# Two sums moved to the vector engine, sample rows in four strips, and sample scores padded to 128 rows, in a two-layer decoder trunk

## The reference

```python
shift, scale, gate = split(silu(c) @ w_ada + b_ada, 3)
x = x + gate * rmsnorm(branch(rmsnorm(x, g_pre) * (1 + scale) + shift), g_post)
```

```python
qk  = einsum(q, k) * dmat                        # scores, with decay
num = a * einsum(q, S) + einsum(qk, v)           # state rows and score rows
den = a * einsum(q, n) + sum(qk)                 # the same two parts, summed
h   = num / maximum(abs(den), exp(-m))
hn  = h * rsqrt(mean(h * h) + eps) * g_head
```

## Time and profile before

| | |
|---|---|
| median of 3 runs | 2228.76 us (2226.25 to 2232.56) |
| time of the profiled execution | 2226.1 us |
| its span in the trace | 2224.5 us |
| PE busy | 2144.5 us, 96% of the span |
| DVE, ACT busy | 941.4 us, 676.8 us |
| moved from and to memory | 298.96 MB |

### The profile page before, as it was taken

How to read it: one execution, slowest core, us unless ns; L and a number is a source line. 1 busy time by engine, 2 the same in 40 slices (tenths; PEclk the granted TensorE clock), 3 DMA queues, 4 the chain that set the end, 5 groups by cost and what they waited for, 6 DMA issues and landing times.

```text
span 2224.5 us, 37038 instructions
## 1 busy us (share of the span) xinstructions
PE 2144.5 (96%) x15828; PEld 1866.3 (84%) x15828; DVE 941.4 (42%) x1432; ACT 676.8 (30%) x1137; POOL 75.7 (3%) x126
## 2 busy tenths in 40 slices
PE   5899999999999999997899999999999999999998
PEld 2579989999999856667889999999899999996676
DVE  4344645546465422235433434334243525254224
ACT  4123434435344321225322222222222222223121
POOL 1000000000000100000000000000000000001000
PEclk8899999999999999998999999999999999999999
DMA  8883222232221588854434343453434244519622
GB/s 321 328 286 96 77 61 78 63 92 58 78 59 58 181 309 309 318 198 133 86 79 114 79 114 79 96 87 83 92 100 98 77 88 84 104 59 335 238 81 100
DMA packets 290527, 298.96 MB, mean 134 GB/s; under 512 B 8721, under 2 KB 213769, under 8 KB 288857
## 3 DMA queue, kind: packets, MB, share of 16 engines
q1 hardware_dynamic: 279504, 247.87, 39.7%
q0 software_dynamic: 10576, 48.45, 6.2%
q10 hardware_dynamic: 290, 0.32, 0.1%
HBM read 277.58 MB, written 23.11 MB: 135 GB/s over the span
## 4 chain that ended last, share of the span: by engine, by line
PE 86%; DMA 9%; DVE 2%; ACT 2%; issue 1%; DVEq 0%; ACTq 0%; SPq 0%
PE PJ L913 49%; PE PJ L1197 14%; DMA raw<-in_w_in_mlstm 5%; DMA obuf<-in_w_ada 3%; PE MX L1125 3%; PE PJ L939 3%; PE MX L1054 2%; PE MX L1063 1%; PE MX L1163 1%; PE MX L1077 1%; DMA arena<-in_x_prompt 1%; PE PJ L1219 1%; PE MX L1017 1%; PE MX L1411 1%; ACT w_hi L1472 1%
## 5 line engine op out<-in xcount | busy, mean ns | idle before, releaser
L913 PE MATMUL PJ<-h_hi,w_hi 128*128 128x272 f32 x3200 | 683.0, 295 | 2.4 <-DVE w_lo L1938 2.4
L913 PE MATMUL PJ<-h_hi,w_lo 128*128 128x272 f32 x3200 | 665.3, 290 | 0.0
L913 PE MATMUL PJ<-h_lo,w_hi 128*128 128x272 f32 x3200 | 663.4, 289 | 1.5 <-issue 1.5
L913 PEld LDWEIGHTS PJ<-h_hi,w_hi 128*128 128x128 f32 x3200 | 506.0, 190 | 26.4 <-issue 20.1
L913 PEld LDWEIGHTS PJ<-h_lo,w_hi 128*128 128x128 f32 x3200 | 506.4, 190 | 1.7 <-issue 1.7
L913 PEld LDWEIGHTS PJ<-h_hi,w_lo 128*128 128x128 f32 x3200 | 503.4, 190 | 0.0
L1938 DVE TENSOR_TENSOR w_lo<-raw,w_hi 128x2048 fp32r<-128x2048 f32 x94 | 215.4, 2292 | 305.5 <-ACT w_hi L1472 305.3
L1472 ACT ACTIVATE w_hi<-raw 128x2048 fp32r<-128x2048 f32 x94 | 179.4, 1909 | 57.4 <-DMA raw<-in_w_in_mlstm 42.3
L1197 PE MATMUL PJ<-w_hi,h_hi 128*128 128x512 f32 x448 | 181.5, 405 | 0.0
L1197 PE MATMUL PJ<-w_hi,h_lo 128*128 128x512 f32 x448 | 176.4, 394 | 0.0
L1197 PE MATMUL PJ<-w_lo,h_hi 128*128 128x512 f32 x448 | 176.1, 393 | 0.0
(11 more groups left out here) (396 smaller groups left out, 2231.2 us busy)
## 6 DMA issues: line engine op xcount, KB each, us to landing
arena<-in_w_ada SPq DMA_DIRECT2D x64, 1024.0 KB, 8.8
raw<-in_w_in_mlstm SPq DMA_DIRECT2D x52, 1024.0 KB, 17.1
raw<-in_w_in_attn SPq DMA_DIRECT2D x40, 1024.0 KB, 5.7
obuf<-in_w_ada SPq DMA_DIRECT2D x32, 1024.0 KB, 10.9
raw<-in_w_out_attn SPq DMA_DIRECT2D x16, 1024.0 KB, 12.9
raw<-in_w_out_mlstm SPq DMA_DIRECT2D x16, 1024.0 KB, 5.0
obuf<-in_w_in_mlstm SPq DMA_DIRECT2D x12, 1024.0 KB, 27.2
arena<-in_state_C POOLq DMA_DIRECT2D x8, 1024.0 KB, 15.8
```

Of the source, the lines that this page charges most:

```text
L913: last = mm(PJ[:, 2 * pair + f, 0:HT], w, h[:, k, HT * f:HT * f + HT], start=(k == 0 and n == 0), stop=(k == KT - 1 and n == 2))
```

## The change

- `memory` step 2 on DVE adds the score columns to the state columns of chunks 1 to 3 in `qn`; step 4 on PE then makes the denominators with a product over 128 score columns and one over the 384 summed ones.
- `Ds` becomes 128 rows high, zero below row 32 (one memset in `gate_maxima`), and DVE adds it to `qn[:, TP:T]`.
- After step 5, ACT takes only the left half of the bank, times a mask of the strips' rows, and DVE, in its step 5, adds the right half times the other mask. Step 6 on PE then has one score product and one selecting product for each half, both over 128 rows, and one product for the denominator; it waits on `qs_done`.
- DVE's step 7 first adds the two blocks of squares; step 8 has two products instead of four.
- The 32 sample rows of an output product are laid out in four strips of columns: strip `j` holds column block `j` of each quarter. `sample_sum` and the sample part of `gate_rows` become four products of 128 columns, one for each strip; the latter writes bank 2, so that `strip` waits for `mod_taken` after a gate. Squares and gating of the samples run once per layer over 128 partitions.
- `x_sample`, `g_post` for samples and `y_sample` are moved with four pieces of 512 B for each row instead of one of 2 KB.
- Four semaphores of the first stage become one, with the same order.

```diff
             def strip(landed, j, n):
+                if j == 0 and is_gate(n - 1):
+                    pe.wait_ge(mod_taken, n - 7)
...
             def gate_rows(n):
-                mm(MX[32 * g:32 * g + 32, 1, :], sel[0:MROWS + 1, X_GS:X_GS + TS], rows, start=True, stop=True)\
-                    .then_inc(mod_turned, 1)
+                for j in range(4):
+                    last = mm(MX[32 * j:32 * j + 32, 2, P * g:P * g + P], sel[0:MROWS + 1, X_GS:X_GS + TS],
+                              rows[:, P * j:P * j + P], start=True, stop=True)
+                last.then_inc(mod_turned, 1)
...
             def sample_sum(l, g):
-                mm(MX[32 * g:32 * g + 32, 1, :], sel[:, X_ST:X_ST + TS], scp[:, :], start=True, stop=True)\
-                    .then_inc(ysum_made, 1)
+                for j in range(4):
+                    last = mm(MX[32 * j:32 * j + 32, 1, P * g:P * g + P], sel[:, X_ST:X_ST + TS],
+                              scp[:, P * j:P * j + P], start=True, stop=True)
+                last.then_inc(ysum_made, 1)
...
             def memory(m, p):
-                    mm(MX[:, 2, :], ones, Dm[:, :], start=True, stop=False)
-                    mm(MX[:, 2, P:TP], ones, qn[:, P:TP], start=False, stop=True).then_inc(num_ready, 1)
+                    mm(MX[:, 2, 0:P], ones, Dm[:, 0:P], start=True, stop=True)
+                    mm(MX[:, 2, P:TP], ones, qn[:, P:TP], start=True, stop=True).then_inc(num_ready, 1)
...
-                    pe.wait_ge(qg_done, val(0, 1, m, 1))
+                    pe.wait_ge(qs_done, val(0, 1, m, 1))
                     for blk in range(2):
                         o = MX[:, 3, TS * blk:TS * blk + TS]
-                        mm(o, vs[0:TS, P * blk:P * blk + P], Ds[0:TS, :], start=True, stop=False)
-                        for c in range(2):
-                            mm(o, Dm[:, DV * c + P * blk:DV * c + P * blk + P], fix[:, C_SS + TS * c:C_SS + TS * c + TS],
-                               start=False, stop=(c == 1))
-                    mm(MX[:, 3, 64:64 + TS], ones[0:TS, :], Ds[0:TS, :], start=True, stop=False)
-                    mm(MX[:, 3, 64:64 + TS], ones, qn[:, TP:T], start=False, stop=True)\
-                        .then_inc(nums_ready, 1)
+                        mm(o, vs[:, P * blk:P * blk + P], Ds, start=True, stop=False)
+                        mm(o, Dm[:, P * blk:P * blk + P], fix[:, C_SS:C_SS + TS], start=False, stop=True)
+                    mm(MX[:, 3, 64:64 + TS], ones, qn[:, TP:T], start=True, stop=True).then_inc(nums_ready, 1)
...
-                    pe.wait_ge(hsq_done, val(0, 2, m, 2))
+                    pe.wait_ge(hsum_done, val(0, 1, m, 1))
                     for f in range(2):
-                        for blk in range(2):
-                            last = mm(MX[:, 1 + f, 0:HT], ones, hsq[:, blk, HT * f:HT * f + HT],
-                                      start=(blk == 0), stop=(blk == 1))
+                        last = mm(MX[:, 1 + f, 0:HT], ones, hsq[:, 0, HT * f:HT * f + HT], start=True, stop=True)
...
             def memory(m, p):
-                    fn(Dm, MX[:, 2, :], ACT.Copy).then_inc(qg_done, 1)
+                    fn(Dm[:, 0:DV], MX[:, 2, 0:DV], ACT.Copy, scale=bm[:, NB:NB + 1]).then_inc(qg_done, 1)
...
             def memory(m, p):
+                    dve.wait_ge(P_done, val(0, 1, m, 1))
+                    chain(tt(qn[:, P:TP], qn[:, P:TP], Dm[:, P:TP], ALU.add))
                     cp(nout[:, ds(h + 64, 1)], nn[:, 3:4]).then_inc(S_done, 1)
...
-                    tt(Ds[0:TS, :], Ds[0:TS, :], MX[0:TS, 3, 64:64 + TS], ALU.mult).then_inc(Ps_done, 1)
+                    chain(tt(Ds[0:TS, :], Ds[0:TS, :], MX[0:TS, 3, 64:64 + TS], ALU.mult))
+                    tt(qn[:, TP:T], qn[:, TP:T], Ds, ALU.add).then_inc(Ps_done, 1)
...
+                if p == 5:
+                    dve.wait_ge(qg_done, val(0, 1, m, 1))
+                    stt(Dm[:, 0:DV], MX[:, 2, DV:2 * DV], bm[:, NB + 1:NB + 2], Dm[:, 0:DV], ALU.mult, ALU.add)\
+                        .then_inc(qs_done, 1)
...
                 if p == 7:
+                    dve.wait_ge(hsq_done, val(0, 2, m, 2))
+                    tt(hsq[:, 0, :], hsq[:, 0, :], hsq[:, 1, :], ALU.add).then_inc(hsum_done, 1)
```

More of the change, by code:

```diff
@@ L108 @@
 C_OH, C_O3, C_SS = 305, 313, 337
-C_FIX = C_SS + 2 * TS
+C_FIX = C_SS + TS
 C_NEGD, C_NEGS = C_FIX, C_FIX + 768
@@ L698, in _ @@
                     sp.wait_ge(xs_ready, 2)
-                    for g in range(4):
-                        sp.dma_start(y_sample.rearrange("b t d -> (b t) d")[:, 512 * g:512 * g + 512],
-                                     xs[32 * g:32 * g + 32, :]).then_inc(y_out[1], 16)
+                    for j in range(4):
+                        sp.dma_start(y_sample.rearrange("b t (g j c) -> (b t) j g c", g=4, j=4)[:, j],
+                                     xs[32 * j:32 * j + 32, :].rearrange("p (g c) -> p g c", g=4)).then_inc(y_out[1], 16)
             sp.wait_ge(y_out[0], 16 * 8)
@@ L948, in _ @@
             tr(MX[:, 2, 0:80], gvec, ident[0:80, 0:80]).then_inc(vec_ps, 1)
-            pe.wait_ge(ct_rows, 1)
+            pe.wait_ge(ct_steps, 2)
             for k in range(KT):
                 last = tr(MX[:, 3, NSEQ * k:NSEQ * k + NSEQ], c_rows[:, P * k:P * k + P], ident[0:NSEQ, 0:NSEQ])
-            last.then_inc(ct_ps, 1)
-            pe.wait_ge(ct_ready, 1)
+            last.then_inc(ct_steps, 1)
+            pe.wait_ge(ct_steps, 4)
             def turn_x(t):
@@ L1117, in _, with strip @@
             layer0("l0z", it0, (None, GR - 1))
-            def strip(landed, j):
+            def strip(landed, j, n):
                 at = fixed(pe, landed)
-                pe.wait_ge(ct_ready, 1)
+                if j == 0 and is_gate(n - 1):
+                    pe.wait_ge(mod_taken, n - 7)
+                pe.wait_ge(ct_steps, 4)
                 pe.wait_ge(u_in[j], at)
@@ L1271, in _ @@
             pe.wait_ge(sc_s, 1)
-            for c in range(4):
-                last = tr(MX[:, 0, :].rearrange("p (g c t) -> p g c t", g=4, c=4)[:, :, c, :],
-                          ys[:, P * c:P * c + P], ident)
+            for g in range(4):
+                last = tr(MX[:, 0, P * g:P * g + P], ys[:, P * g:P * g + P], ident)
             last.then_inc(t_samp, 1)
@@ L1456, in _ @@
             act.wait_ge(c_in, 32)
-            fn(c_tanh, c_rows, ACT.Tanh, scale=0.5).then_inc(ct_tanh, 1)
+            fn(c_tanh, c_rows, ACT.Tanh, scale=0.5).then_inc(ct_steps, 1)
             def round_hi(ph, it, e, j=0):
@@ L1526, in _ @@
             row_squares(0)
-            act.wait_ge(ct_ps, 1)
+            act.wait_ge(ct_steps, 3)
             act.wait_ge(const_in, 16)
-            fn(cT[:, 0:KT * NSEQ], MX[:, 3, 0:KT * NSEQ], ACT.Copy).then_inc(ct_ready, 1)
+            fn(cT[:, 0:KT * NSEQ], MX[:, 3, 0:KT * NSEQ], ACT.Copy).then_inc(ct_steps, 1)
             row_root(0)
@@ L1671, in out_square, with sample_square @@
                 act.wait_ge(y_sq, 16 * l + 4 * g + t)
-                act.wait_ge(ysq_s, 4 * l + g + (t > 1))
+                act.wait_ge(ysq_s, l + (g == 3 and t > 1))
                 fn(jk, PJ[:, bank_of(l, t), :], ACT.Square, accum_out=st[:, 4 * t + g:4 * t + g + 1]).then_inc(y_sq, 1)
-            def sample_square(l, g):
-                rows = slice(32 * g, 32 * g + 32)
-                act.wait_ge(ysum_made, 4 * l + g + 1)
-                act.wait_ge(y_sq, 16 * l + 4 * g + 2)
-                fn(jk[rows, :], MX[rows, 1, :], ACT.Square, accum_out=st[rows, 16:17]).then_inc(ysq_s, 1)
+            def sample_square(l):
+                act.wait_ge(ysum_made, 4 * l + 4)
+                act.wait_ge(y_sq, 16 * l + 14)
+                fn(jk, MX[:, 1, :], ACT.Square, accum_out=st[:, 16:17]).then_inc(ysq_s, 1)
             def out_root(l, nth, t):
@@ L2379, in gate_maxima @@
                 chain(dve.memset(Rt[0:GP.stop, :], 0.0))
+                chain(dve.memset(Ds, 0.0))
                 chain(dve.memset(tg[:, 0:1], 0.0))
```

58 lines of the change are left out of this document (27 added, 31 removed).

## The result

The median after is 2192.78 us (2188.76 to 2197.3, four runs) against 2229.94 us of the kernel before beside it (2226.25 to 2232.56, four runs). The ratio is 0.983, with a 95% interval from 0.9807 to 0.9853. The forecast was 2193 us, in a range from 2184 to 2208.

A forecast was written before the change was run, and what follows sets the result against it. PE, at work for 96% of the span, was taken as the bound. Savings of 10.0 + 5.1 + 6.9 + 4.8 + 4.2 = 31.0 us plus 5 for the clock, off the 2228.76 us median, gave 2193 us, range 2184 to 2208.

The forecast's parts named there:

- Step 6: Score and selecting products on PE: 2.36 us become 1.1, saving 10.0 us over eight heads; 7.1 by number of records.
- Step 4: Product over `Dm` on PE: 0.86 us becomes 0.22 over 128 columns, saving 0.64 a head, 5.1 us for eight.
- Step 8: Sums of squares on PE: eight records become four, saving 0.86 us a head, 6.9 us for eight.
- the sign named in the prediction: Heads in the changed trace come 2.7 to 2.8 us closer together, if loads keep up.
- Gates and sample sums: Four narrow products on PE overlap across strips: 0.6 us saved each, 4.8 us for eight gates, 4.2 for seven sums.
- The last sum of `out0`: Sample sum after the last strip, where the residual waits for the `x_prompt` reload: its 0.6 us saving is not counted.
- The sum: All savings of PE time without the clock: 31.0 us, with a low bound of 19.1.
- The clock: Half-speed stretches behind step 6 in three of eight heads mostly go: 5 us saved, bounds 0 and 6.8.
- the rule weighed in the prediction: Throttling follows an idle engine, so step 6 is not the cause; second rival, 2198 us, chance 0.18.
- DVE's covers: New DVE work stays hidden: 1.7 us left ahead of step 6, and 2.48 us against 0.72 ahead of step 8.
- The weight loads: ACT waited for weights in `raw` three times from 1131 to 1990 us, 15.2 us in all, 11.4 once.
- The fourth rival: Layer 1's weight loads become the last wait, so heads can't get shorter: 2220 us, chance 0.08.

The follow-up runs named there:

- scores32: The changed kernel with the two score products of step 6 on 32 rows, as before the change; one execution took 2188.99 us.
- sums_only: The kernel before with only the two sums of steps 4 and 8 moved to DVE; 2215.74 us, ratio 0.9969 to the kernel before.
- one_strip: The changed kernel with the four narrow products of each gate and sample sum all in one strip; one execution took 2196.70 us.
- fold_only: The kernel before with only the folded step 6, the padded scores and the merged semaphores; 2210.53 us, ratio 0.9952 to the kernel before.
- fold_sums: The kernel before with the folded step 6 and the two sums on DVE, without the four strips; 2186.14 us, ratio 0.9807 to the kernel before.
- strips_only: The kernel before with only the sample rows in four strips, steps 2 to 8 as before; 2222.51 us, ratio 0.9987 to the kernel before.
- late_short: The changed kernel with two extra multiplications (1.4 to 1.5 us forecast) on DVE directly before the new addition of step 5; one execution took 2192.81 us.
- late_long: The changed kernel with a long reciprocal (about 3.5 us forecast) on DVE directly before the new addition of step 5; it took 2210.76 us.
- second pair: Repeat traces of both kernels without new edits: the kernel before took 2228.54 us, the changed kernel 2183.03 us (median).
- experiment 5: The changed kernel with the `x_prompt` reload in four pieces, 2180.70 us, ratio 0.9799; beside it both kernels again, changed 2183.03 us (0.9816), before 2228.54 us.
- experiment 6: The run `fold_sums`: the kernel before with the folded step 6 and the two sums on DVE, without strips; 2186.14 us against 2229.70, ratio 0.9807.
- before_again: The kernel before, unchanged, profiled once more; it took 2228.54 us.

## Why the prediction was right

The base, the bound and the mechanism held, and the total, 36 us forecast against 37 measured, is right; that it is so close is partly luck, as told below. By its steps:

- *Step 6*, 1.25 us a head: it is 1.33. The choice between 10.0 and 7.1 us was the choice between two prices of a 32-row group, and `scores32` settled it for the higher.
- *Step 4*, 0.64: distances from step 4 to step 6 shrank by 0.71 (17.94 to 17.23). `sums_only`, which has the shorter sum and the old step 6, shows 0.65 of it (17.30); the rest goes with the fold, whose step 6 no longer begins with a change to 32 rows. *Step 8*, 0.86: from step 8 to the next step 4 it is 0.91. The three make 2.98 us a head, 23.8 in eight, where 22.0 were summed; the sign named in the prediction was 2.7 to 2.8.
- *Gates and sample sums*, 0.6 each: a gate's four products take 0.33 us, a little over the 0.29 read off the twelve narrow ones, and a sum's 0.22; together 4.40 us over seven in `out0` and 5.0 over eight in `out1`, so 0.63 each. `one_strip` shows that it is the overlap. The last sum of `out0` saved nothing, as said: the wait for the reload stands at 4.0 us beside 4.1.
- *The sum*: 33.2 us by distances against 31.0. It was 7% too small, each term a little, step 6 the most: its 1.33 lies above the larger of the two prices, 1.25.
- *The clock*, 5 us, bounds 0 and 6.8. Behind step 6 the granted clock went to 0.50 in 15 of 32 heads of the four profiled kernels with the old step 6 (3, 2, 6 and 4), and in none of 72 heads of the nine profiled kernels with the new one on time. A drop costs a head 1.5 us, so some 6 us an execution. `scores32`, with its 1.47 us of step 6, shows none either. That the old step 6 is the cause is shown by `fold_only` and `fold_sums` against `sums_only` and `strips_only`; what exactly it is about 2.36 us of small products is not. The idle time of the rule weighed in the prediction isn't needed. What counts is the stretch ahead of a fall, which the earlier trace rows does not show: in 13 of the 15 PE is busy for all of it, in the first head of the kernel before as follows (PE, PEld, DVE, ACT, POOL, clock, DMA share, GB/s). In the other two, both a fourth head, it is busy for 2.54 and 2.31 of 3.4 us.

```profile
1161.00:1164.40 3.40, 3.40 (x26) 3.05 (x24) 0.00 (x0) 0.00 (x0) 0.00 (x0) 1.00 0.00 0
1164.40:1167.80 3.40, 3.40 (x16) 3.40 (x17) 0.77 (x3) 1.41 (x3) 0.00 (x0) 0.50 0.00 0
```

- *DVE's covers*: 1.7 us forecast ahead of step 6, 1.77 found; 1.8 forecast ahead of step 8 (2.48 less 0.72), 1.84 found. `late_short` and `late_long` bracket the first from both sides.
- *The weight loads*. The prediction read the earlier trace rows as all of ACT's waits for weights. The same view has one more, 8.0 us for a piece that lands in `obuf`, so four pieces were late and not three. After the change five pieces in `raw` and two in `obuf` are.
- *The fourth rival*, weights of layer 1 as the last wait, may be true of one head. From step 4 of the fourth head to that of the fifth there are 116.6 to 124.9 us in folded kernels and 122.3 to 129.8 in the others, in every execution more than in the heads next to it. Loads issued there need 44.2 us (median) to land in the changed kernel, against 17.3 in the second head. DMA issues of the changed kernel (count, KB each, median us to landing), from 1500 to 1570 and from 1250 to 1320 us:

```profile
raw<-in_w_in_mlstm SPq DMA_DIRECT2D x3, 1024.0 KB, 44.2
```

```profile
raw<-in_w_in_mlstm SPq DMA_DIRECT2D x4, 1024.0 KB, 17.3
```

and its waits from 1131 to 1990 us, for the earlier trace rows:

```profile
ACT w_hi L1471 <- DMA raw<-in_w_in_mlstm: 21.0, 5, 12.4
...
PE MX L1359 <- DVE arena L2430: 2.1, 1, 2.1
PE PJ L913 <- DVE w_lo L1935: 2.1, 1, 2.1
```

  That head gave 0.85 us in the first pair of traces and 5.5 in the second. From the waits it is likely that part of its gain hangs on when those loads land, but no experiment shows it; I priced it as one rival of six and not as a fixture of one head.

What the prediction didn't see is the noise of other stages. In the first pair of traces layer 0 took 4.75 us more after than before, for no reason in the change, and the span shrank by 30.6 us where the stages behind layer 0 show 35.9. In the second pair layer 0 went the other way, and the span shrank by 46.2. The ratios, 0.983 (38 us) here and 0.9816 (41 us) in experiment 5, lie between. Three comparisons have each their own executions of the kernel before: the medians differ by 37 us here, by 44 in experiment 5, and by 44 in experiment 6, which has only two of the three parts. That the forecast met the first to 0.2 us is thus partly luck; what the traces bear out is the sum of its terms.

Open is the strips' share of the median. Their 9.4 us stand in the distances of every kernel that has them. The transition behind them does not give it back: it averages 177.8 us in the eight traces with strips and 178.0 in the six without (`one_strip` among these). Yet no median shows the whole of it.

## What to carry to other kernels

Where the matrix engine is the bound, price a small product by the distance from its start to the next start, and count each change between 32 and 128 rows as a cost of its own; padding to 128 rows was cheaper than being exact. When work moves to another engine, compute the cover from the end of the new work to the start of the waiting one, and note that a wait of 1.5 us on the matrix engine cost as much again through the clock in six of eight heads. Judge parts of a change of 1% by the stage distances of the traces: the times of the parts, each known to within 4 us, added up to half of the whole. When you look for what brought the clock down, read the stretch ahead of the fall and not the slow one.

## What the runs showed of the hardware that was not expected

- In layer 0's attention, where all kernels run the same code, the clock fell in three places 136.5 us apart in six of 14 profiled executions, in one place in one, and in none in seven. A set of three costs some 4.5 us, and both kernels have executions of either kind. PE was busy for all of such a stretch, but not ahead of it: it had waited 1.2 us for DVE. The first fall in `before_again`, and the same place in the trace of the kernel before, which has the wait and no fall:

```profile
190.50:193.90 3.40, 2.33 (x15) 1.27 (x16) 1.02 (x3) 0.00 (x0) 0.00 (x0) 1.00 0.70 184
193.90:197.30 3.40, 3.40 (x18) 3.40 (x17) 2.81 (x4) 0.00 (x0) 0.00 (x0) 0.50 0.00 0
```

```profile
191.10:194.50 3.40, 2.35 (x15) 1.30 (x16) 1.02 (x3) 0.00 (x0) 0.00 (x0) 1.00 0.67 183
194.50:197.90 3.40, 3.40 (x29) 3.40 (x29) 2.80 (x5) 0.00 (x0) 0.00 (x0) 1.00 0.00 0
```

  So a short wait stands ahead of these falls as in `late_long`, and does not always bring one. What decides is open.
- Added idle time of 1.4 to 1.5 us ahead of step 6 brought the clock down in six of eight heads; the new step 6 without it, at 1.03 us or at the 1.47 of `scores32`, did so in none of 72.
- Loads of the fourth head's weights are slow for both kernels and the experiments: 36.8 to 44.3 us to land, at the median, in 11 of the 14 traces and 28.7 to 29.6 in the other three, against 17.3 in the second head of the changed kernel. No experiment was made on the cause, and it is open.
